# Key pages of the paged attention moved into the input projection, and prompt heads interleaved with the samples' value pages in four column groups

## The reference

```
def _ab_mixer(x, w_in, ..., w_out, past_k, past_v):
    h = x @ w_in
    u_a, v_a, q, k, v = split(h)                       # 5 x 512 features
    a_out = _chunk_gmlp(gelu(u_a), layer_norm(gelu(v_a)), w_s, b_s)
    b_out = _sb_self(q, k, v) or _sb_decode(q, k, v, past_k, past_v)
    return concat([a_out, b_out]) @ w_out, k, v, v_a

def _sb_weights(z, causal):                            # stick-breaking attention
    log_keep = where(causal, -softplus(z), 0)
    suffix = cumsum(shifted log_keep, reverse)
    return where(causal, exp(log_sigmoid(z) + suffix), 0)

def _sb_decode(...):                                   # per sample, 8 heads of 64
    z = concat([q @ past_k, q @ k]) * scale + bias
    a = _sb_weights(z, kpos < qpos)
    out = a[..., :P] @ past_v + a[..., P:] @ v
```

## Time and profile before

| | |
|---|---|
| median of 3 runs | 1987.19 us (1985.29 to 1987.68) |
| profiled execution, its own time | 1992.15 us |
| its span | 1990.3 us |
| TensorE matmuls busy | 94% of the span |
| VectorE, ScalarE, GpSimd busy | 45%, 26%, 8% |
| attention loop and what it needs | first loop matmul at 171.64 us, output projection of layer 0 from 446.13 us |

### The profile page before, as it was taken

How to read it: one execution, slowest core, us unless ns; L and a number is a source line. 1 busy time by engine, 2 the same in 40 slices (tenths; PEclk the granted TensorE clock), 3 DMA queues, 4 the chain that set the end, 5 groups by cost and what they waited for, 6 DMA issues and landing times.

```text
span 1990.3 us, 35549 instructions
## 1 busy us (share of the span) xinstructions
PE 1878.3 (94%) x13522; PEld 1652.8 (83%) x13522; DVE 901.2 (45%) x1442; ACT 524.0 (26%) x738; POOL 154.0 (8%) x119
## 2 busy tenths in 40 slices
PE   8898999999899999997998998998998799999996
PEld 8895555649799999997976976976976699999996
DVE  3634333424655335545327227227227655335543
ACT  3322222211322122223222222222223422222222
POOL 0200000000100000000501301301301200000000
PEclk9998999999899999998999999999999999999998
DMA  5446777742122322221234324334324123222321
GB/s 187 164 132 201 243 249 254 221 138 74 43 84 88 102 74 84 92 99 43 81 116 143 100 111 148 95 111 148 95 111 153 52 85 100 89 74 88 99 91 45
DMA packets 83912, 234.23 MB, mean 118 GB/s; under 512 B 9617, under 2 KB 9778, under 8 KB 83490
## 3 DMA queue, kind: packets, MB, share of 16 engines
q1 hardware_dynamic: 83138, 228.26, 35.1%
q0 software_dynamic: 736, 5.48, 0.7%
HBM read 209.90 MB, written 23.80 MB: 117 GB/s over the span
## 4 chain that ended last, share of the span: by engine, by line
PE 83%; DVE 4%; ACT 2%; DMA 1%; issue 1%; DVEq 0%; SPq 0%; ACTq 0%
PE banks L1173 62%; PE banks L1247 5%; PE banks L1218 3%; PE banks L1360 2%; PE banks L1440 2%; PE banks L1432 1%; PE banks L1278 1%; PE banks L1269 1%; PE banks L1288 1%; PE banks L1420 1%; DVE x_lo L946 1%; DMA s<-in_s 1%; DVE y L925 1%; PE banks L1281 1%; DMA out_ret_s<-s 1%
## 5 line engine op out<-in xcount | busy, mean ns | idle before, releaser
L1173 PE MATMUL banks<-x_hi,w_hi 128*128 128x272 f32 x2624 | 550.3, 291 | 42.3 <-DVE x_lo L946 28.1
L1173 PE MATMUL banks<-x_hi,w_lo 128*128 128x272 f32 x2624 | 547.1, 290 | 0.0
L1173 PE MATMUL banks<-x_lo,w_hi 128*128 128x272 f32 x2624 | 545.7, 290 | 0.0
L624 DVE TENSOR_TENSOR w_lo<-w_raw,w_hi 128x1024 fp32r<-128x1024 f32 (+2 forms) x228 | 287.2, 1259 | 516.2 <-ACT w_hi L425 516.0
L425 ACT ACTIVATE w_hi<-w_raw 128x1024 fp32r<-128x1024 f32 (+2 forms) x228 | 238.4, 1045 | 1028.1 <-PE banks L1173 1001.4
L1173 PEld LDWEIGHTS banks<-x_hi,w_hi 128*128 128x128 f32 x2624 | 416.4, 190 | 47.9 <-issue 28.6
L1173 PEld LDWEIGHTS banks<-x_lo,w_hi 128*128 128x128 f32 x2624 | 417.1, 191 | 0.0
L1173 PEld LDWEIGHTS banks<-x_hi,w_lo 128*128 128x128 f32 x2624 | 414.2, 191 | 0.0
L1173 PE MATMUL banks<-act_hi,w_lo 128*128 128x272 f32 x704 | 145.3, 287 | 0.0
L1173 PE MATMUL banks<-act_lo,w_hi 128*128 128x272 f32 x704 | 145.1, 287 | 0.0
L1173 PE MATMUL banks<-act_hi,w_hi 128*128 128x272 f32 x704 | 145.1, 287 | 0.0
(11 more groups left out here) (224 smaller groups left out, 1810.3 us busy)
## 6 DMA issues: line engine op xcount, KB each, us to landing
w_raw<-in_w_up SPq DMA_DIRECT2D x88, 512.0 KB, 3.5
kv<-in_kc SPq DMA_DIRECT2D x128, 256.0 KB, 4.1
kv<-in_vc SPq DMA_DIRECT2D x128, 256.0 KB, 3.7
w_raw<-in_w_rin SPq DMA_DIRECT2D x48, 512.0 KB, 3.5
w_raw<-in_w_dn SPq DMA_DIRECT2D x32, 704.0 KB, 4.0
s<-in_s SPq DMA_DIRECT2D x32, 512.0 KB, 7.1
out_ret_s<-s SPq DMA_DIRECT2D x32, 512.0 KB, 2.7
w_raw<-in_w_in_ab SPq DMA_DIRECT2D x20, 512.0 KB, 3.7
```

The costliest lines, as they stand in the source:

```text
L624: V.tensor_tensor(w_lo[:, j, 0:k * P], w_raw[:, j, 0:k * P], w_hi[:, j, 0:k * P].bitcast(F32), ALU.subtract).then_inc(lo_ready, 1)
L1173: last = mm(B[:, 2 * j + half, 0:HN], a[:, j, w], x[:, kt, half * HN:(half + 1) * HN], start=kt == 0 and n == 0, stop=kt == k - 1 and n == 2)
```

## The change

- The projection's tiles come in the order q, k, gate v, v, u and all 20 are written out. From tile 4 on, half a sample's key pages (8 pages, a quarter of the slots' 16 pages twice over) are multiplied after each tile: 16 halves after tiles 4 to 19. `qk` now takes four pages in one matmul of 512 columns, and its neighbours in order alternate between two column groups.
- SP issues 8 pages behind each weight tile, then the value pages, in halves.
- The scores of all 8 samples are kept (`z_low`, and four of them in `y`), and `z_rows`, `z_columns`, `dec_z` run between tiles. Transposes, gate-v statistics and the new keys' scores are spread over tiles 12 to 19.
- The loop has only value pages: turn n does `pr_qk` of head n+1, `av` of sample n, whose pages go to column groups 0, 1, 2, 3 in turn, `pr_suffix`, `suffix` of sample n+1, and so on. `zp`, `lp`, `ld`, `ad` are doubled; the copies `qpair`, `kpair`, `vpair` are gone.
- GpSimd no longer multiplies the residual; VectorE does it in the add of the output projection (`scale=True`).

```diff
+            def load_half(q):
+                cache = A["kc"] if q < 2 * DEC_B else A["vc"]
+                first = HALF * (q % 2)
+                pages = page_ids(q // 2 % DEC_B, first)
+                if q >= 2:
+                    sp.wait_ge(kv_used, q - 1)
+                for s in range(first, first + HALF):
...
+            for u in range(6, N_IN_AB):
+                load(A["w_in_ab"], u, U_IN_AB + u, u % 2, KD)
+                load_half(u - 4)
...
+            for q in range(N_IN_AB - 2, 4 * DEC_B):
+                load_half(q)
...
-            nc.gpsimd.tensor_scalar(y[:, :, :], y[:, :, :], ALPHA, None, ALU.mult).then_inc(y_scaled, 1)
...
+            def qk(q):
+                b, first = q // 2, HALF * (q % 2)
...
+                for c in range(4):
+                    for r in range(first // 2, (first + HALF) // 2):
+                        last = mm(B[32 * r:32 * r + 32, 4, :], qz[:, b, c, :],
+                                  view(kv[:, 2 * r, 0, :], (512, 4), (1, P), off=c * P), start=c == 0, stop=c == 3)
+                last.then_inc(kv_used, 1)
...
+            for u in range(N_IN_AB):
+                tile_in(u)
...
+                if u >= 6 and u % 2 == 0:
...
+                    z_columns((u - 6) // 2)
...
+                if u >= 4:
+                    qk(u - 4)
...
+                    mm(B[0:TS, 7, :], an[:, b, :, :].rearrange("p c h -> p (c h)"), v_nat[0:TS, NB, :], start=True, stop=False)
+                for s in range(first, first + HALF):
+                    pe.wait_ge(kv_landed[s], 32 * (DEC_B + b) + 32)
+                    for g in range(PER_SLOT):
+                        k, r = divmod(PER_SLOT * s + g, 4)
+                        last = mm(B[32 * r:32 * r + 32, 7, :], ad[:, b % 2, :, 4 * r + k], kv[:, s, g, :],
+                                  start=k == 0 and r > 0, stop=k == 3)
...
+            for n in range(H_B):
+                if n + 1 < H_B:
+                    pr_qk(n + 1)
+                av(2 * n)
+                pr_suffix(n)
+                if n + 1 < DEC_B:
+                    suffix(n + 1)
+                av(2 * n + 1)
+                pr_av(n)
+                av_columns(n)
...
+            for n in range(H_B):
+                if n:
+                    dec_out(n - 1)
+                if n + 1 < H_B:
+                    pr_z(n + 1)
+                pr_zr(n)
+                if n + 1 < DEC_B:
+                    dec_zr(n + 1)
+                    pr_sp(n + 1)
+                dec_rows(n)
+                if n + 2 < DEC_B:
+                    dec_sp(n + 2)
+                if n % 2:
+                    pair_out(n // 2)
```

More of the change, by code:

```diff
@@ L280, in load_kv @@
[L280 to L296, removed]
@@ new lines, in va_stats, with va_variance @@
+            def va_stats(first, end):
+                for t in range(first, end):
+                    dve.wait_ge(cop_a, t + 1)
+                    step.add(V.bn_stats(vst[0:rows_of_block(t), t, :], va_nat[0:rows_of_block(t), t, :]))
+            def va_variance():
+                step.wait()
+                for t in range(NB + 1):
+                    last = V.bn_aggr(vmv[0:rows_of_block(t), t, :], vst[0:rows_of_block(t), t, :])
+                    if t < NB:
+                        step.add(last)
+                last.then_inc(va_var, 1)
@@ new lines, in va_shift, with copy_v @@
+            def va_shift():
+                step.wait()
+                for t in range(NB + 1):
+                    rows = rows_of_block(t)
+                    V.tensor_tensor(va_nat[0:rows, t, :], va_nat[0:rows, t, :], vlnb[0:rows, :], ALU.add)\
+                        .then_inc(va_ready, 1)
+            def copy_v(first, end):
+                for t in range(first, end):
+                    dve.wait_ge(nat_b, t + 1)
+                    V.tensor_copy(v_nat[0:rows_of_block(t), t, :], B[0:rows_of_block(t), 5 + t % 2, :])\
+                        .then_inc(cop_b, 1)
@@ new lines, in _ @@
+            for pr in range(4):
+                mix_gate(pr)
+            dve.wait_ge(chunk_stored, 16)
+            step.add(V.memset(smask[:, :, :], 1.0))
+            step.wait()
+            step.add(V.memset(smask[:, :, 0:1], 0.0))
+            dec_sp(0)
+            pr_z(0)
+            for pr in range(4):
+                dve.wait_ge(gm_hi, pr + 1)
+                V.tensor_tensor(x_lo[:, pr, :], uT[:, pr, :], x_hi[:, pr, :].bitcast(F32), ALU.subtract)\
+                    .then_inc(gm_lo, 1)
@@ new lines, in av_columns, with z_bank, r_bank @@
+            def av_columns(b):
+                pe.wait_ge(o_rows_ready, b + 1)
+                for c in range(4):
+                    last = mm(B[:, 7, c * 8:(c + 1) * 8], o_rows[:, c * P:(c + 1) * P], quad[:, c * 8:(c + 1) * 8],
+                              start=True, stop=True)
+                last.then_inc(o_done, 1)
+            def z_bank(j):
+                bank, first = ((0, 0), (1, 0), (2, 0), (1, 384))[j]
+                return B[:, bank, first:first + CAUSAL[j]]
+            def r_bank(j, c0, w):
+                bank, first = ((3, 0), (4, 0), (2, 0), (4, 384))[j]
+                return B[:, bank, first + c0:first + c0 + w]
@@ new lines, in pr_av @@
+            def pr_av(n):
+                c, h2 = divmod(n, 2)
+                rows = slice(64 * h2, 64 * h2 + 64)
+                pe.wait_ge(pa_ready, n + 1)
+                if h2 == 0 and c:
+                    pe.wait_ge(po_lo, c)
+                for j in range(NB):
+                    last = mm(B[rows, 5, j * P:TP], v_nat[:, j, c * P + 64 * h2:c * P + 64 * h2 + 64],
+                              zp[n % 2][:, PZ[j]:PZ[j] + CAUSAL[j]], start=j == 0, stop=j == NB - 1)
+                last.then_inc(pav_done, 1)
@@ L1341, in _ @@
+            pr_qk(0)
             pe.wait_ge(gm_out, 4)
+            z_columns(DEC_B - 1)
+            suffix(0)
             pe.wait_ge(an_ready, 1)
[L1344 to L1350 removed]
+            pe.wait_ge(z_ready, DEC_B)
+            for n in range(H_B):
+                if n + 1 < H_B:
+                    pr_qk(n + 1)
+                av(2 * n)
+                pr_suffix(n)
+                if n + 1 < DEC_B:
+                    suffix(n + 1)
+                av(2 * n + 1)
+                pr_av(n)
+                av_columns(n)
```

766 lines of the change are left out of this document (377 added, 389 removed).

## The result

The changed kernel takes 1903.07 us (median of 4 runs, 1900.14 to 1904.81); the kernel before took 1986.59 in the same rounds. The ratio is 0.9578, with a 95% interval of 0.9562 to 0.9595. Forecast were 1885.5 us and a gain of 101.7; the gain is 83.5. The time is 18 us above the forecast: it lies in the 8-in-10 range (1872 to 1922), and 3 us above the forecast's own range (1872 to 1900). The profiled execution took 1903.15 us, so it can be read as the median.

What follows compares the result with a forecast made beforehand. TensorE was taken to bound the kernel. Projection to 197.6, bridge 18, loop 124.8 and 4 for waits start the output projection at 344.4, 101.7 earlier: 1885.5 us, own range 1872 to 1900, 8-in-10 range 1872 to 1922.

Steps and rivals of the forecast that it cites:

- pages at 250 GB/s: Case of slower transfers in projection and loop: slots of 10.5 us, turns of 16.8, total 1908.
- The four groups: Page matmuls in different column groups run together: a `qk` half takes 3.6 us, an `av` half 1.84.
- The 75 in the forecast: The part of the 101.7 us gain expected from faster `av` in the loop.
- the rival with chance 0.20: Transfers pace key slots and loop turns: 1908 us at 250 GB/s, 1952 at 218; chance 0.20.
- Step 1, the projection: Input projection of layer 0 with key pages between its tiles: ends at 197.6 us, the 6.22 us stall gone.
- it is loaded nearly two slots (19 us) ahead of its use: In the projection, a weight tile queued behind the wait for `kv_used` still comes early enough.
- Step 2, the bridge: Stretch between projection and attention loop, following VectorE: about 18 us.
- Step 3, the loop: Attention loop: seven turns of 15.75 us, a last of 11.5, and 3 for handovers, 124.8 together.
- the 3 us for handovers: Allowance in the loop's sum, 0.4 us a turn.
- The chain's rival (0.14): VectorE and ScalarE pace the loop, 3 us late each turn, 24 in all: 1910 us; chance 0.14.
- the 4 us for early waits: Added for waits at the key stage's start, where constants, weights and pages share the queues.
- the residual's edit: GpSimd's residual multiplication goes, VectorE's add takes it over: the projection's 6.22 us stall goes, gain about 6.

Runs made afterwards that it cites:

- Run 7: The changed kernel with every value page written to column group 0 again; 1987.62 us, ratio 0.9999 to the kernel before.
- Run 8: The changed kernel with the two loops of `qk` swapped, four matmuls of one column group in a row, then four of the other; 1925.89 us.
- run 1: The changed kernel with each weight tile of the projection issued one slot earlier, ahead of the pages that stood before it; 1897.38 us.
- run 2: The changed kernel with 2, 4 and 5 extra matmuls, whose results nobody reads, filling TensorE's waits in the bridge; 1901.39 us.
- run 5: The changed kernel with weight tiles one slot earlier and one block of `pr_suffix` ahead of the next `pr_qk`, without filler matmuls; 1892.87 us.
- its repetition: The changed kernel measured again without an edit; 1905.93 us, ratio 0.9600 to the kernel before.
- run 3: The changed kernel with three of the four blocks of `pr_suffix` moved ahead of the next `pr_qk`; 1900.56 us.
- Run 4: The changed kernel with the first block of `pr_suffix` moved ahead of the next `pr_qk`; 1899.68 us.
- run 6: The changed kernel with weight tiles one slot earlier, one `pr_suffix` block ahead of `pr_qk`, and 2, 4 and 9 filler matmuls in the bridge; 1881.75 us.
- run 9: The kernel before with one part of the change alone: `av` writes four column groups and `av_columns` adds them; 1966.84 us, ratio 0.9910.

## Why the prediction was right, and where it was short

The mechanism was right, and the time came out 18 us late. That it lies in the 8-in-10 range is in part luck: the range reached to 1922 for pages at 250 GB/s and for a late chain, and neither came. What took the room was mostly the granted clock, which is in no term and no rival of the prediction.

**The four groups, right.** `qk` halves take 3.56 (3.6 forecast), `av` halves 1.88 (1.84), undisturbed turns 15.75 (15.75 without handovers). Run 7 takes the overlap of `av` away and loses 84.6 us (79.6 at the output projection's start); by the forecast's pieces it is 8 x (14.0 - 3.7) = 82. The 75 in the forecast is this less the 0.98 a turn for the new rows, which stay in run 7, as the four matmuls of `av_columns` do. Run 8 takes a part of the overlap of `qk` and loses 22.8.

**Transfers, right.** 261 and 266 GB/s are sustained, where the earlier trace rows were the only sign; the rival with chance 0.20 didn't come about.

**Step 1, the projection, 7.6 too short.** Two terms failed. First, "it is loaded nearly two slots (19 us) ahead of its use": the tile is issued so, but it lands 8.7 us after its issue, and ScalarE stands waiting for such tiles 121.8 us in all. Its first use isn't TensorE's: `w_hi` on ScalarE and `w_lo` on VectorE read it, and `w_lo` stands in order ahead of the copies that TensorE needs sooner. That gives the stall of 3.65 and some 1.7 of half clock behind it; run 1 takes both away. Second, the change between pages and full-width tiles was put into the 3.6 of a half; the tile has one at each end. A slot is 0.16 longer than 9.6, and 0.08 where `z_columns` or transposes stand between, 1.8 in all. The Trainium skill (TensorEngine Tiling (Array Packing), Key Properties) says that changing the tiling mode drains the array. The trace agrees at the tile's end: its last pair takes 0.34 to the next start when pages follow (70.36 to 70.70) and 0.25 when `z_columns` of the tile's own mode do (60.16 to 60.41). At its beginning the trace doesn't tell: the first pair takes 0.35 behind pages, but also 0.33 behind `av_columns` (362.38 to 362.71), where the mode stays. Together 3.65 + 1.7 + 1.8 = 7.15; the first half of pages also starts 0.5 late.

**Step 2, the bridge, 1.5 too short.** It follows VectorE as forecast. Part of TensorE's work there runs at half clock, from 216 on, but that isn't what makes it long: with the fillers alone it takes 19.8 (run 2), with the weights first and no fillers 17.8 (runs 1 and 5). What goes with the weights is the wait of 1.01 for `z` at 209.32. In six profiled executions with the weights of the change (it, its repetition, runs 2, 3, 4 and 7) this wait is 0.58 to 1.46, and the bridge is 18.5 plus the wait in each. So these 1.5 us go with the order of the weights too; which of VectorE's instructions carry them on was not taken apart.

**Step 3, the loop, 12.9 too short.** The term that was missing is the granted clock. The sum took every piece at full clock, as the earlier trace rows show the loop of before (0.98). In the change the first turn carries the bridge's half clock on (19.97, 4.2 more than a clean turn), and falls inside later turns cost 3.3 (19.03 - 15.77), 1.6 and 1.6 (17.38 each) and, by the granted clock from 332 to 340, 3.4: 9.9 together. Waits inside the loop add 1.6, and the 3 us for handovers weren't needed: 124.8 + 4.2 + 9.9 + 1.6 - 3 = 137.5. Run 4, which only alters the order, makes the loop 8.7 shorter (225.50 to 354.48, 128.98); run 6, with the bridge filled too, 124.0. The chain's rival (0.14) said 1910, nearer to the measured time than the forecast, but for the wrong cause: TensorE's 1.6 us of waits are all that it had.

Of the 4 us for early waits little was needed: TensorE waits 1.2 us from 20 to 60, and the stall came later and from another cause. That they were added hides 4 of the 22 us by which the three steps are short. And the residual's edit was worth 8 to 11 in the kernel before instead of 6, which doesn't enter the sum, as this was built up from pieces.

The kernel with weights first, another order and a filled bridge takes 1881.75, 3.8 below the forecast, with the three parts near those of the sum.

## What to carry to other kernels

Matmuls with weights of 32 columns run fully side by side here when neighbours in program order belong to different column groups (run 8 loses half of the overlap), and the gain arrives only if the order leaves VectorE time for what comes next (run 9). When TensorE's work shrinks, look at the clock that a stretch is granted: the stall of 3.65 us cost 5.35 and that of 6.22 cost 8.4, and a row of narrow products lost up to 3.4 us in a turn without any wait. Here a full-width block placed between the narrow products ended that. Time a weight tile's load by the first engine that reads it, not by TensorE.

## What the hardware showed that was not expected

- The granted clock fell to half with TensorE busy in every microsecond: 0.51 from 247.4 to 254.1, behind `pr_av` (64 of the array's columns), `av_columns` (8 moving columns) and `pr_qk` (64 of the array's rows). The same sequence also passed at 1.00 (279.46). With full-width products between `av_columns` and `pr_qk`, seven turns in each of four runs kept 1.00 from the second turn on. The Trainium skill (TensorE: Matmul & The Clock Gate, HAM oscillation — how this bites in real kernels) puts such falls down to waits between bursts of matmuls, there for transfers. The bridge is only in part in keeping with it: the clock falls at 216.4 behind waits of 1.01 and 1.43, but narrow products stand there too, and the longer waits (2.08 and 2.54) come after the fall. The turns are not, as no wait stands there. What in the narrow products brings the fall on was not taken apart.
- A row of four matmuls in one group and then four in the other takes 5.3 us a half. If only the last of one group and the first of the other ran side by side, it would be 7 x 0.876 = 6.1; so some of the overlap reaches further.
- Pages of 256 KB, with weight tiles between them, kept 261 GB/s for 145 us, and pages alone 268 for 107 us of run 4's loop, where the loop of before moved 218.
